# Query block 2 and key block 2 taken as a third pair of seven half products, in a float32 encoder on one core

## The reference, cut to what matters

```python
D_MODEL = 1024; D_POOL = 256; D_MLSTM = 768; N_HEADS = 4; HEAD_DIM = 192
def trunk(x, ...):                 # two sequences: 16 + 256 and 16 + 1024 tokens
    h = rmsnorm(x, norm1_g)
    z = h @ w_in                   # 1024 -> 256 (u) + 768 (q) + 768 (k) + 768 (v) + 768 (o) + gates
    qk = silu(centred_dwconv(z[..., 256:1792], conv_w, conv_b))    # 3 taps along the tokens
    y = concat(pool_mixer(u), mlstm_mixer(q, k, v, o, gates))
    x = x + y @ w_out
    x = x + expert_choice_ffn(rmsnorm(x, norm2_g))    # 16 experts, each 164 tokens
    return rmsnorm(x, final_g)
```

## Time and profile before

| | |
|---|---|
| median of three runs | 1695.24 us |
| the profiled execution: its time | 1694.48 us |
| its span, first to last instruction | 1692.7 us |
| mean granted TensorE clock | 0.995 |
| TensorE (PE) busy | 1659.8 us, 98% |
| VectorE (DVE) busy | 504.2 us, 30% |
| ScalarE (ACT) busy | 412.2 us, 24% |
| GpSimd (POOL) busy | 511.4 us, 30% |
| longest wait of TensorE in the mixer | 2.9 us, for ScalarE's L1011 |

### The profile page before, as it was taken

The page is one execution under the profiler, slowest core; times in us unless marked ns, Lnnn a source line. Parts: engine busy times, 40 slices in busy tenths (PEclk is TensorE's granted clock), DMA queues, the critical chain, the costliest instruction groups (busy, mean ns, idle before and its releaser), DMA issues.

```text
span 1692.7 us, 25643 instructions
## 1 busy us (share of the span) xinstructions
PE 1659.8 (98%) x10365; PEld 1417.5 (84%) x10365; DVE 504.2 (30%) x1081; ACT 412.2 (24%) x937; POOL 511.4 (30%) x461
## 2 busy tenths in 40 slices
PE   9999999999999999999999999999999999999996
PEld 6555688867869874455999999999999999999996
DVE  5573424682223650079211101111011110111105
ACT  3335234323232534464011011100111011110115
POOL 0073042671210444342131323313233123322220
PEclk9999999999999999999999999999999999999998
DMA  9310113321110636434588778877888778787794
GB/s 293 99 54 6 70 39 80 93 94 38 38 32 17 201 86 231 143 107 158 191 279 286 234 249 280 287 268 236 267 261 303 252 235 287 241 316 239 234 311 190
DMA packets 189812, 309.83 MB, mean 183 GB/s; under 512 B 12645, under 2 KB 77973, under 8 KB 189617
## 3 DMA queue, kind: packets, MB, share of 16 engines
q1 hardware_dynamic: 171840, 283.30, 48.4%
q0 software_dynamic: 17904, 25.62, 7.5%
HBM read 275.82 MB, written 33.07 MB: 182 GB/s over the span
## 4 chain that ended last, share of the span: by engine, by line
PE 91%; DVE 5%; ACT 1%; issue 1%; DMA 1%; SPq 0%; POOL 0%; DVEq 0%; ACTq 0%; POOLq 0%
PE bank L2434 33%; PE bank L2451 16%; PE bank L2171 8%; PE bank L2192 6%; PE bank L2146 6%; PE bank L2338 5%; PE bank L2064 3%; PE bank L2100 2%; PE bank L2268 2%; PE bank L2249 1%; DVE arena L1833 1%; DVE arena L1831 1%; DVE arena L1835 1%; PE bank L2110 1%; PE bank L2108 1%; PE bank L2471 1%
## 5 line engine op out<-in xcount | busy, mean ns | idle before, releaser
L2434 PE MATMUL bank<-arena 128*128 128x164 f32 x4096 | 573.0, 303 | 0.5 <-DVE arena L1940 0.5
L2434 PEld LDWEIGHTS bank<-arena 128*128 128x128 f32 x4096 | 570.8, 190 | 0.7 <-DVE arena L1940 0.7
L2451 PE MATMUL bank<-arena 128*128 128x164 f32 x1920 | 269.7, 303 | 0.0
L2451 PEld LDWEIGHTS bank<-arena 128*128 128x128 f32 x1920 | 268.0, 190 | 0.0
L960 POOL DMA_INDIRECT residual<-arena,cur_scatter x90 | 140.7, 1563 | 180.1 <-ACT arena L1431 157.2
L1950 DVE TENSOR_TENSOR arena<-bank,arena 128x328 f32<-128x328 f32 x64 | 32.0, 500 | 527.5 <-ACT arena L1420 517.8
L2338 PE MATMUL bank<-arena 128*128 128x512 f32 x320 | 146.1, 599 | 0.8 <-issue 0.7
L1420 ACT ACTIVATE arena<-bank 128x328 f32<-128x328 f32 x64 | 28.4, 443 | 480.5 <-PE bank L2434 436.7
L2171 PE MATMUL bank<-arena 128*128 128x192 f32 x840 | 137.7, 326 | 2.9 <-ACT arena L1011 2.9
L2171 PEld LDWEIGHTS bank<-arena 128*128 128x128 f32 x840 | 136.5, 189 | 3.6 <-issue 3.1
L945 POOL COPY cur_gather<-idx_q 128x6 uint32 (+1 forms) x15 | 2.8, 189 | 370.4 <-DVE arena L1945 353.7
(11 more groups left out here) (275 smaller groups left out, 1643.2 us busy)
## 6 DMA issues: line engine op xcount, KB each, us to landing
arena<-in_w_up SPq DMA_DIRECT2D x32, 2048.0 KB, 12.8
arena<-in_w_down SPq DMA_DIRECT2D x32, 2048.0 KB
arena<-in_w_gate SPq DMA_DIRECT2D x32, 2048.0 KB, 7.8
arena<-in_w_in SPq DMA_DIRECT2D x7, 1536.0 KB, 6.6
arena<-in_x_sample SPq DMA_DIRECT2D x14, 512.0 KB, 5.2
arena<-x_features_first SPq DMA_DIRECT2D x11, 512.0 KB, 7.6
arena<-decay_rows SPq DMA_DIRECT2D x22, 256.0 KB, 4.7
arena<-state_rows SPq DMA_DIRECT2D x44, 128.0 KB, 4.2
```

The source lines that it names most:

```text
L2434: last = pe.matmul(ps[2 * w + fp % 2][:, a * SLOTS:(a + 1) * SLOTS], ring[2 * (fp // 2) + w][:, k, f * P:(f + 1) * P], xeT[:, k, 0:SLOTS], ...
L2451: last = pe.matmul(result_tiles(4 + dp % 2)[:, a, 0:SLOTS], ring[4 + dp // 2][:, k, dt * P:(dt + 1) * P], hidT[:, k, :], start=k == 0, sto ...
```

## The change

- **A third pair.** q2 and k2, whose weights lie in two different slots, are taken together by seven half products. `PAIRS` names the three pairs g = 0, 1, 2: (q0, q1), (q2, k2), (k0, k1). Round 0 makes q0 and q1 alone as before, then pairs 1 and 2; round 1 makes pairs 0, 1, 2, all before the gates and the values, which then follow each other.
- **Another order of the phases in a pair:** A1, A2, F1, B, E1, E2, F2 (`PAIR_PHASES`).
- **Sums.** GpSimd makes the sums of weights of pairs 1 and 2 of round 0 one after the other, of (1, 1) after T4, (1, 2) after pair (1, 0); those of the values of round 1 after the last gate is opened. VectorE makes the sums for pair (1, 0) between T1 to T4, at the end of round 0 (`query_sums`), before the reciprocal on which L873 waits. ScalarE copies out A1 of pair (1, 0) before it squares the last tile of round 0.
- **Loads.** In round 1 the order of the blocks is q, k, gates, v in place of q, gates, k, v.
- **Banks.** The phases of a kind use banks (0, 6), (1, 7), (2, 4), (3, 5) in place of (n, n + 4), and the short tile has bank 7 in place of one of banks 0 to 3.
- VectorE adds the taps of a pair's second block before the combinations of F2, and those of its first block after them (pairs 0 and 1) or in the steps of the gates or values (pair 2).

```diff
@@ bank_plan @@
+PAIR_PHASES = ("A1", "A2", "F1", "B", "E1", "E2", "F2")
+BANKS_OF = {"A": (0, 6), "B": (1, 7), "E": (2, 4), "F": (3, 5)}
...
-            b = "ABEF".index(key[-1 if key[0] == "sv" else 3][0]) + 4 * (key[4] if key[0] == "sq" else key[3] % 2)
+            b = BANKS_OF[key[-1 if key[0] == "sv" else 3][0]][key[4] if key[0] == "sq" else key[3] % 2]
+        if key[0] == "vo":
+            b = BANKS_OF["B"][1]
@@ encoder_program @@
-        CONV = [(0, 0, 0), (0, 0, 1), (0, 0, 2), (0, 1, 1), (0, 1, 0), (0, 1, 2), (1, 0, 2), (1, 0, 1), (1, 0, 0), (1, 1, 1), (1, 1, 0), (1, 1, 2)]
+        PAIRS = (((0, 0), (0, 1)), ((0, 2), (1, 2)), ((1, 0), (1, 1)))
+        CONV = [(0, 0, 0), (0, 0, 1)] + [(p, *PAIRS[g][n]) for p in range(2) for g in range(1 - p, 3) for n in (1, 0)]
@@ gpsimd @@
+                        pair_sums(0, 1)
+                        pair_sums(0, 2)
...
+                            open_gate(t + HALF_TILES)
-                            if t == 1:
-                                key_sums(1)
-                        value_sums(1)
+                        tile_sums(1, 0, 8, 11)
...
                     pool.wait_ge(y_raw, NT)
-                    query_sums()
+                    pool.wait_ge(halves_ready, 12)
+                    pair_sums(1, 1)
                     pool.wait_ge(rs_ready, 1)
@@ scalar @@
+                def first_products(p, g):
+                    act.wait_ge(taps_done, CONV.index((p, *PAIRS[g][1])))
                     for c, (lo, hi) in enumerate(HALF_CHUNKS):
                         at = 2 + HALF_AT + lo
+                        evac(("sq", p, g, "A1", c), Z_of[0][:, at:at + hi - lo], lambda b: b[:, 0:hi - lo])
...
+                    for g in range(1 - p, 3):
+                        first_products(p, g)
+                        if (p, g) == (1, 0):
+                            last_norm(0)
+                        first_quarter(p, g)
+                        if g > 1 - p:
+                            silu(p, *PAIRS[g - 1][0])
+                        centre_pair(p, g)
@@ vector @@
                         combine(key("E2", c), Z_of[1][:, 1 + c + lo:1 + c + hi], later(0, c)[:, 0:hi - lo], lambda b: b[:, 0:hi - lo])
+                    outer_taps(p, *PAIRS[g][1], Z_of[1])
                     for c in range(2):
                         combine(key("F2", c), later(0, c), later(0, c), lambda b: b[:, 0:width[c]])
...
+                    for g in range(1 - p, 3):
+                        combine_pair(p, g)
+                        if g < 2:
+                            outer_taps(p, *PAIRS[g][0], Z_of[0])
...
                     mean_of(late)
+                    if p == 0:
+                        query_sums()
                     dve.wait_ge(rms_ready, 2 * p + 1)
@@ tensor @@
-                        block_alone(0, 0, 2)
...
-                        block_alone(1, 0, 2)
-                        block_pair(1, 0)
-                        tokens_by_block(1, 1, 6)
-                    block_pair(p, 1)
-                    block_alone(p, 1, 2)
+                    for g in range(1 - p, 3):
+                        block_pair(p, g)
+                    if p:
+                        tokens_by_block(1, 1, 7)
                     tokens_by_block(p, 0, 4 + 4 * p)
```

More of the change, by code:

```diff
@@ L1122, in centre_pair @@
                         read_out(act, key)
-                    for j, x in ((1, "E2"), (0, "F2")):
+                def centre_pair(p, g):
+                    if (p, g) == (0, 1):
+                        act.wait_ge(ypool_out, 32)
+                    for n, x in ((1, "E2"), (0, "F2")):
                         for c in range(2):
-                            read_out(act, ("sq", p, w, x, c))
-                        centre(p, w, j, Z_of[j])
+                            read_out(act, ("sq", p, g, x, c))
+                        centre(p, *PAIRS[g][n], Z_of[n])
+                    silu(p, *PAIRS[g][1])
                 def first_values(p, t):
@@ L1264, in _ @@
                         values_of(p, t)
-                        if t == 2:
-                            silu(p, 1, 2)
+                        if p == 0 and t == 1:
+                            silu(0, *PAIRS[2][0])
                     for n, i in enumerate(range(NT - 1, -1, -1)):
@@ L1625, in outer_taps @@
                         outer_tap(p, w, j, n_tap, Z)
[L1626 removed]
+                    if n in (0, 2):
                         st.do(dve.memset(qkT[w][:, :, LEN:T], 0.0))
@@ L1798, in _ @@
                         dve.sem_inc(hh_ready, 1)
+                    if p == 0:
+                        for n in range(2):
+                            clear_borders(n)
+                    late = slice(2 * EARLY * p, 2 * NT)
                     dve.wait_ge(hh_sq, 2 * (p + 1) * NT)
-                    late = slice(2 * EARLY * p, 2 * NT)
                     mean_of(late)
+                    if p == 0:
+                        query_sums()
                     dve.wait_ge(rms_ready, 2 * p + 1)
@@ new lines, in block_pair @@
+                def block_pair(p, g):
+                    one, two = (Wb[(2 + 3 * p + w) % 2][:, :, j * P:(j + 1) * P] for w, j in PAIRS[g])
+                    s1, s2, s4 = sums_k[g % 2]
+                    early, late = slice(0, 4), slice(4, 8)
+                    operands = {"A1": (one[:, early], hT[:, early, 0:HALF]), "B": (s2, T2), "F1": (s1, T1), "E1": (two[:, early], T3),
+                                "A2": (one[:, late], hT[:, late, 0:HALF]), "E2": (two[:, late], T4), "F2": (s4, hT[:, late, HALF_AT:LEN])}
+                    for w, j in PAIRS[g]:
+                        nb = 2 + 3 * p + w
+                        pe.wait_ge(w_slot_in[nb % 2], 16 * (nb // 2 + 1))
+                    halves = {"F1": 1, "B": 2, "E1": 3, "E2": 4}
+                    if (p, g) == (1, 0):
+                        halves = {"F1": 6, "B": 8, "E1": 10, "E2": 11, "F2": 12}
+                    for x in PAIR_PHASES:
+                        if x == "F1" and (p, g) != (1, 0):
+                            pe.wait_ge(sums_ready, SUMS_PAIR[p, g])
+                        if x == "F1" and (p, g) == (1, 0):
+                            pe.wait_ge(own_free[0], (NT + 1) // 2)
+                        if x in halves and g == 1 - p:
+                            pe.wait_ge(halves_ready, halves[x])
@@ L2167, in tokens_by_block @@
                                 pe.wait_ge(sums_ready, sums + 1)
+                            if t == 0 and x == "F2":
+                                pe.wait_ge(sums_ready, sums + 2)
                             b = bank(("sv", p, w, t, x))
```

230 lines of the change are left out of this document (93 added, 137 removed).

## The result

| | before | changed |
|---|---|---|
| median of the runs, us | 1694.74 | **1720.84** |
| lowest to highest | 1693.88 to 1695.87 | 1719.66 to 1722.14 |
| profiled execution: its time / its span | 1694.48 / 1692.7 | 1721.58 / 1719.7 |

A forecast was written before the change was run, and what follows sets the result against it. TensorE, busy 98% of the span, was taken as the bound, so its waits add. Savings -10.3, waits +27.7 and clock +3.4 gave +20.8 on the profiled 1694.48: 1715.3, as a median 1716.0 us, range 1703 to 1725.

The forecast's parts named there:

- What is saved: TensorE: two new pairs save 3.72 us each, and the 2.88 us wait behind the short tile goes; together 10.3 us.
- The border of (q2, k2) to (k0, k1): Where this pair follows a pair, TensorE waits for A1 to be copied out: 4.3 us in round 0, 4.2 in round 1.
- VectorE's taps, 3.5, to +8.2: Border chain: the first block's taps take 3.5 us, ending 8.2 us after TensorE ends the previous pair.
- The border behind the first pair of round 1: TensorE waits 11.0 us there, as GpSimd's scaling of the gates, taken as 7.7 us, holds up VectorE's taps.
- the rival without that: Scaling and taps do not meet at round 1's first border: it costs 4.2 in place of 11.0; 1707.5 us, chance 0.10.
- pooled features: After the gate rows of round 0, the fifth matmul waits for ScalarE's first copy, so A1 starts 2.5 us later.
- first pair of round 1: At the start of round 1, F1 waits 1.2 us for VectorE's first sum of weights.
- values of round 0: ScalarE's silu of k1 stands ahead of the short tile's copies, so A1 leaves its bank late: 0.7 us.
- values of round 1: GpSimd's sums of the values' weights follow the last opened gates, so TensorE waits 3.8 us for B.
- All waits together: Sum of TensorE's predicted waits: 19.5 at the borders, then 2.5, 1.2, 0.7 and 3.8, giving 27.7 us.
- The clock: TensorE's lower clock costs two losses of 1.7 us, behind the 11 us wait and one around 4 us: 3.4 us.
- The rival in which the clock falls at every wait of 2.4 us or more: Six clock losses of 1.7 us in place of two: 1722.8 us, chance 0.04.

The follow-up runs named there:

- old borders: The changed kernel, but the three pairs that stand behind another pair run in the order A1, B, F1, E1, A2, E2, F2 again; 1691.40 us.
- GpSimd silent: The changed kernel, but GpSimd holds back its weight sums and the scaling of the gates until the taps of the pair in question are done; 1710.81 us.
- the longer fill: The changed kernel with 26, 36 and 20 needless TensorE matmuls of 272 columns behind A1 at the three borders; 1728.42 us.
- values' sums earlier: The changed kernel, but GpSimd makes the first two sums of round 1's value weights before it opens the last tile of gates; 1715.77 us.
- old order in all pairs: The changed kernel with all five pairs, the first of each round too, in the order A1, B, F1, E1, A2, E2, F2; 1700.28 us.
- the shorter fill: The changed kernel with 15, 21 and 12 needless TensorE matmuls of 272 columns at the three borders, just inside the waits; 1713.91 us.
- the other bank: The kernel before with one edit: the short tile of gates or values goes to the second bank of the B products; 1692.08 us.

## Why the prediction was right, and where its steps were off

The sign, the mechanism and each place of a wait held. The size, 1716.0 against 1720.84, was low, nearly all of it by the clock. By its own steps:

- **What is saved: held.** Two pairs for two times 3.72 us, and the 2.88 behind the short tile (2.9 to 3.0 measured by itself). A pair at the full clock is 31.72 us, as before (63.45 for two in the kernel with old borders).
- **The border of (q2, k2) to (k0, k1): mis-sized.** The term was 4.3 in round 0 and 4.2 in round 1; measured 7.34 and 5.73. The step that failed is "VectorE's taps, 3.5, to +8.2", the first block's taps behind F2: they took 6.18 and 5.02, while the second block's took the 3.46 of their step. GpSimd's sums of the value weights start at 196.12, as their load lands, in the middle of them. In round 1 the gates' weights do the same at 439.47, in the taps that begin at 437.59. The prediction took this clash into account only for the scaling. The meeting is built into the order: the load of these weights is issued when a pair's last product has left their buffer (189.64 and 432.93 in SyncE's timeline), and GpSimd begins 6.5 us later both times, while the taps of that same pair run from about 5 us after that moment on. With GpSimd silent, 4.62 and 4.18, which is the term as worked out.
- **The border behind the first pair of round 1: 11.0 against 10.00.** The scaling took 7.24 us (7.7 was taken), and the taps began when its end was 3.3 us away. Scaling and taps did meet, so the rival without that fell; kept apart in an experiment they leave 4.20, its number.
- **The small waits:** pooled features 2.5 against 2.21, first pair of round 1 1.2 against 1.00 (the first sum of weights took 0.69, 0.7 was taken), values of round 0 0.7 against 0.22, values of round 1 3.8 against 3.32. All waits together 27.7 against 29.8; that this is close is in part luck, as 4.6 us too little at two borders stand against 2.5 too much at the other places.
- **The clock: the term that was most wrong.** Two losses of 1.7 us, 3.4, against five of together 9.8. The step that failed was to read the earlier trace rows as a threshold in the length of the wait: the clock stayed up over 2.88 us in the old trace, so waits around 4 us were counted as half safe. In all the traces of this case every wait of TensorE of 3.3 us or more after the program's first 20 us, 16 of them in seven kernels, has the lower clock behind it. Shorter waits go both ways: the 2.88 us did not bring it, and the 2.21 us at the pooled features, with the same work ahead of them, have it behind them in three traces (the change, the longer fill, values' sums earlier) and not in three others (old borders, old order in all pairs, GpSimd silent). In two more (the shorter fill, the other bank) the clock falls at that place ahead of any wait. What decides there, no run took apart. The Trainium skill ("TensorE: Matmul & The Clock Gate", Part 1) says that the lower clock is the default and that activity releases it; the trace agrees in that the clock was low behind each long wait and rose again while TensorE worked.
- **Not foreseen:** the drop at the start of the experts (810 us in the old trace) is gone, -1.7 us, though nothing there was changed. It is absent from five of the ten traces and present in the others, the kernel before with the other bank among them. A trace is one execution, and executions of one kernel differ too: the 19 of the kernel before beside the first experiments took 1693.15 to 1697.05 us, with mean clocks of 0.995 for the shortest and 0.993 for the longest. What moves such a drop is open.

Terms against measurement: +2.1 of waits, +6.4 of clock, -1.7 at 810 us, together +6.8 on 1715.3, and the profiled execution took 1721.58. The rival in which the clock falls at every wait of 2.4 us or more, 1722.8, was nearest to what happened. It counted six losses, but only five waits of the prediction are that long (2.5, 4.3, 11.0, 4.2 and 3.8), which makes 1721.1; and of the five drops that came, the one at the pooled features stood behind 2.21 us.

## What to carry to other kernels

A product that adds onto another in the same bank needs that one copied out first; what stands between the two is cover for the copy. Reordering to hide late inputs at a pipeline's start takes cover away at every later repetition, so choose the order per instance, not for all: here the new order is worth 8.9 us at the start of round 1 and costs 29.4 at three borders. Price a long wait of TensorE at its length and the slow clock behind it (here 6.9 us on 23.1), and for each VectorE step on the chain ask which GpSimd instruction may become ready during it, those released by a load among them.

## What the runs showed of the hardware beyond what was expected

- The length of a short wait does not tell whether the clock falls: behind one and the same wait of 2.21 us it was 0.57 in the changed kernel and 1.00 in the one with old borders, and behind 2.88 us in the old trace 1.00. Behind every wait of 3.3 us or more it was low. With TensorE kept busy through three waits it stayed at 2.4 GHz and gave back 6.9 us.
- A matmul of 272 columns in f32 took 0.465 us when issued back to back, though a single record of it lasts 0.39 us: each is two instructions in the trace, and their records overlap. Sizes of a fill are to be read from a run's length by its count, not from one record.
- Taps of 3.46 us took up to 9.26 us beside GpSimd, while a sum of GpSimd that takes 1.09 us alone (at 379.65) took 1.97 beside them: both engines lose, as each waits for the other's instruction to end.
